# Inverse roots by Ln and Exp from one table set, without reciprocals on VectorE, and another order of steps, in a hybrid decoder layer

## The reference

```python
def rms_norm(x, g):
    y = x * rsqrt(mean(x * x, axis=-1) + 1e-6)
    return y * g
# ssd: y (T, 512) of a Mamba-2 scan, times silu(z)
# nsa: 8 query heads x 64, 2 KV heads; three branches (means of blocks of 32, selected
#      blocks, a window of 512), each a masked softmax; mixed by sigmoid gates, times silu(z)
mix = concat(rms_norm(ssd, ssd_norm_g), rms_norm(nsa, att_norm_g))   # (T, 1024)
x = x + gate * (mix @ w_out)
y = rms_norm(x, final_g)
```

## Time and profile before

| | us |
|---|---|
| median of 3 runs | 929.72 |
| lowest, highest | 928.70, 930.92 |
| the profiled execution, its whole time | 924.17 |
| its span, first to last instruction | 922.40 |

### The profile page before, as it was taken

The page is one execution under the profiler, slowest core; times in us unless marked ns, Lnnn a source line. Parts: engine busy times, 40 slices in busy tenths (PEclk is TensorE's granted clock), DMA queues, the critical chain, the costliest instruction groups (busy, mean ns, idle before and its releaser), DMA issues. The chain is left out here.

```text
span 922.4 us, 18991 instructions
## 1 busy us (share of the span) xinstructions
PE 855.8 (93%) x8117; PEld 499.1 (54%) x8117; DVE 455.9 (49%) x954; ACT 353.4 (38%) x714; POOL 201.0 (22%) x174
## 2 busy tenths in 40 slices
PE   2999999999999999999899998789898989899887
PEld 1454674455566655667455555545556564654553
DVE  1133131052535355446554536886886868667511
ACT  3041000210201044555343236775665656454523
POOL 1001766000200033334410110137210130303021
PEclk9999999999999999999999999789999999999989
DMA  8937137322220000120844541720011010102102
GB/s 281 351 122 280 62 131 248 157 92 91 92 93 0 1 6 0 36 57 1 308 149 130 165 165 35 233 63 27 14 47 50 13 54 18 61 3 69 60 2 91
DMA packets 44461, 88.98 MB, mean 96 GB/s; under 512 B 4196, under 2 KB 25900, under 8 KB 43034
## 3 DMA queue, kind: packets, MB, share of 16 engines
q1 hardware_dynamic: 39354, 56.02, 18.7%
q0 software_dynamic: 5024, 31.75, 9.5%
HBM read 75.49 MB, written 16.40 MB: 100 GB/s over the span
## 5 line engine op out<-in xcount | busy, mean ns | idle before, releaser
L1798 PE MATMUL PS<-hT,W 128*128 128x363 f32 (+1 forms) x384 | 118.6, 469 | 0.0
L1778 PE MATMUL PS<-W,hT 128*128 128x512 f32 x256 | 113.0, 594 | 0.5 <-DVE W L1428 0.5
L1798 PEld LDWEIGHTS PS<-hT,W 128*128 128x128 f32 x384 | 72.2, 189 | 45.6 <-issue 1.7
L1595 DVE CUSTOM_DVE_ANT_0 PS<-PS,consts 128x640 f32<-128x640 f32 (+5 forms) x96 | 77.4, 836 | 29.0 <-PE PS L2107 28.5
L1728 PE MATMUL PS<-W,hT 128*128 128x288 f32 (+1 forms) x256 | 86.5, 500 | 0.0
L1778 PEld LDWEIGHTS PS<-W,hT 128*128 128x128 f32 x256 | 47.9, 190 | 56.3 <-issue 54.8
L886 POOL TENSOR_TENSOR Q<-Q,U 128x512 f32<-128x512 f32 x16 | 20.3, 1266 | 265.8 <-DVE U L1629 265.8
L1728 PEld LDWEIGHTS PS<-W,hT 128*128 128x128 f32 x256 | 48.5, 190 | 37.4 <-issue 30.7
L1155 ACT ACTIVATE hT<-PS,small 128x128 f32<-128x128 f32 (+7 forms) x64 | 46.9, 740 | 49.9 <-DVE small L1595 47.0
L2074 PE MATMUL PS<-U,Y 128*128 128x512 f32 x128 | 60.3, 603 | 0.8 <-ACT OTb L1162 0.8
L2074 PE MATMUL PS<-U,Q 128*128 128x512 f32 x128 | 58.8, 598 | 0.0
(11 more groups left out here) (457 smaller groups left out, 1538.9 us busy)
## 6 DMA issues: line engine op xcount, KB each, us to landing
W<-in_w_in SPq DMA_DIRECT2D x5, 2048.0 KB, 7.9
W<-in_w_ada SPq DMA_DIRECT2D x8, 1024.0 KB, 11.1
U<-in_x_prompt SPq DMA_DIRECT2D x8, 512.0 KB, 7.6
W<-in_w_ada SPq DMA_DIRECT2D x2, 2048.0 KB, 8.0
U<-in_state_win_kv POOLq DMA_DIRECT2D x8, 512.0 KB, 4.9
W<-in_x_prompt SPq DMA_DIRECT2D x8, 512.0 KB, 3.3
out_y_prompt<-W SPq DMA_DIRECT2D x8, 512.0 KB, 2.8
out_new_win_sample<-in_state_win_kv POOLq DMA_DIRECT2D x1, 4032.0 KB, 24.0
```

Of the source, the lines that this page charges most:

```text
L1595: ins = nc.vector.tensor_tensor_reduce(x, x, strip(u), 1.0, -NEG, ALU.add, ALU.min, sneg_m[u % 2][:, m:m + 1])
L1778: ins = nc.tensor.matmul(bank(z_bank(u)), hT3[:, k, i * P:(i + 1) * P], w, start=(k == 0), stop=(k == KT8 - 1))
L1798: ins = nc.tensor.matmul(bank(b, 0, n), w[:, k, ct % 4 * P:ct % 4 * P + P], hT3[:, k, a:a + n], start=(k == 0), stop=(k == KT8 - 1))
```

## The change

It does three things. First, ACT loads, ahead of the stage's first wait, the table set that holds both Ln and Exp. Each inverse root is then computed on ACT alone as exp(-0.5 * ln(scale * x + eps)), in place, by a function `inverse_root`, with a wait for its own instruction after each of the two. Second, DVE's reciprocals, and the semaphores between ACT and DVE for them, go; the final norm's root is no longer taken at a GATE two tiles on or at a ROOT step but at the FINAL itself, and the step h is gone. For the last tile, DVE still adds eps to the first half's sum (now under the semaphore `s_eps_added`) and waits for the finished inverse root. Third, the order of all the steps is another. The diff, without the two hunks that rename and remove semaphores:

```diff
@@ -616,26 +615,26 @@
         LAST_TURN = {UNITS[us[0]][0:2]: n for n, us in enumerate(TURNS)}
 
         MIX = [TT] + list(range(TT))
-        OUTPUT = ("GATE", "SCALE", "TURN", "OUT", "RES", "SQUARE", "ROOT", "FINAL")
+        OUTPUT = ("GATE", "SCALE", "TURN", "OUT", "RES", "SQUARE", "FINAL")
 
 
         NAMES = {"q": "QT", "z": "SAMPLE", "s": "S", "x": "SOFTMAX", "t": "TURNP", "y": "CT", "w": "CV", "v": "PV", "k": "BACK",
-                 "c": "COPY", "m": "SUM", "g": "GATE", "a": "SCALE", "u": "TURN", "o": "OUT", "r": "RES", "n": "SQUARE", "h": "ROOT", "f": "FINAL",
+                 "c": "COPY", "m": "SUM", "g": "GATE", "a": "SCALE", "u": "TURN", "o": "OUT", "r": "RES", "n": "SQUARE", "f": "FINAL",
                  "p": "WGATE"}
         ORDER = (
-            "qqssxsxyxwmtsvcxtqksysxvxcszsxxwkgstmstxvvcsaxykuwsxtmootooogaxtoooqtssrrvxppvctxtskusvxtpvxsvc"
-            "sxoxspsotppxpoxqpkttsnsyorxoogxottosrvvvttcxsknxavsvvvcstxtuwsxxoqsstmkoxxftosstxoxossgoxtxooyrs"
-            "rvxvssfvtvxcaxstxwmkussxxvvststvvxxvsscxqkxosxtosnsoyxosxtstooxwxssrtgoxxossmrxvvxvsastvvtcx"
-            "xkussvvxxtnsxvssfxvsxxsxvyvsstcoxxqwossmotoxosxgstttoxroxaokssrnxvvxvsstvvctxxkussfxvvtvsxvs"
-            "xvxvvssctooxtsxgtxsoxorkssxvvvxsxvvcatytssoxouoxoftrssoxkoooxsnsrwtxoxossgomxxorasxvvstsvvfx"
-            "vtstvxxvvctkuvvnvvvcokoooorogoauofrooonhofroooornhf")
+            "qsqxsxyswxsxstmvcxstqxkzvttcskgasuvvcyoxxowstomxktossxogooxoptarpprquspsvxxtvttspcksxvpxvvcsystxwoso"
+            "gxsmaotpxxypktostooxtssrxtqxonotsrvvvscxtxukwsmxsvxvvsvsxcsototxsxfgstxaoooxtstsxxtotkroossnrxvvvyvx"
+            "cstxkusxsvvvxstsvvxstcxxqostxsoxwsftsxoxosnmsxxorgqtksxsoooyxtsrfsxvvxstasvvxvscxtxkwmusxsvvxssvxxst"
+            "xsvnxvtvcssxooxgtssxxytqooasxstoxsfortxokosrnxvtvsxsvvvxstcsxkusvxxvsvgsvxtxvssxxvvscsttwxomoyxftosw"
+            "soxmoooarxkotrussvxvxvssxvvscoxkoooogaototorsxtsrxvxvsnsnxvvsxtxsvsxsvtvxxvttcfkvvvfvvcukogoaoourooo"
+            "oornooooroofornf")
 
         VALUE_TILES = [min(u // 2, WIN // P if u % 2 else TT) + 1 for u in range(2 * TT)]
         VALUE_STEPS = [u for u, n in enumerate(VALUE_TILES) for _ in range(n)]
         STEPS, seen = [], {}
         for letter in ORDER:
             m = seen[letter] = seen.get(letter, -1) + 1
-            STEPS.append((NAMES[letter], {"o": m // 8, "r": m // 2, "h": TT - 1 + m, "v": VALUE_STEPS[min(m, len(VALUE_STEPS) - 1)]}.get(letter, m)))
+            STEPS.append((NAMES[letter], {"o": m // 8, "r": m // 2, "v": VALUE_STEPS[min(m, len(VALUE_STEPS) - 1)]}.get(letter, m)))
         AGAIN, times = [], {}
         for step in STEPS:
             AGAIN.append(times.get(step, 0))
@@ -643,7 +642,6 @@
         POS = {(what, u, again): n for n, ((what, u), again) in enumerate(zip(STEPS, AGAIN))}
 
 
-        ROOTED = {step: n + 1 for n, step in enumerate(step for step in STEPS if step[0] in ("SCALE", "FINAL") or step == ("SQUARE", TT))}
         ADDED = {step: n + 1 for n, step in enumerate(step for step in STEPS if step[0] in ("BACK", "SQUARE"))}
         TURNED = {step: n + 1 for n, step in enumerate(step for step in STEPS if step[0] in ("CT", "TURNP"))}
 
@@ -1086,6 +1084,13 @@
                 act.activation(PTs[:, 0:4, :].rearrange("p n r -> p (n r)"), bank(0), ACT.Copy).then_inc(s_turned_act, 1)
                 z_silu(Z_AMID[p])
 
+            nc.scalar.preload_act_table_set("natural_log_exp_and_others")
+
+            def inverse_root(to, x, scale, eps):
+
+                alink(act.activation(to, x, ACT.Ln, scale=scale, bias=eps))
+                alink(act.activation(to, to, ACT.Exp, scale=-0.5))
+
             act.wait_ge(s_smp_sum, 4)
             for (what, u), again in zip(STEPS, AGAIN):
                 tile = MIX[u] if what in OUTPUT else None
@@ -1094,7 +1099,7 @@
                     act.wait_ge(s_ysq, 9)
                     q = ssq.rearrange("p (i s) -> p i s", s=2)[:, :, 0:1]
                     for a, b, n in ((0, TT, P), (TT, TT + 1, SR)):
-                        act.activation(q[0:n, a:b], q[0:n, a:b], ACT.Sqrt, scale=1.0 / SW, bias=eps2[0:n]).then_inc(s_yroot, 1)
+                        inverse_root(q[0:n, a:b], q[0:n, a:b], 1.0 / SW, eps2[0:n])
                 if what == "GATE":
 
                     if u:
@@ -1103,28 +1108,26 @@
                         act.wait_ge(s_smp_gated, 1)
                     q = ssq[0:r, 2 * tile + 1:2 * tile + 2]
                     if u:
-                        alink(act.activation(za[tile], Q3[:, tile, :], ACT.Square, accum_out=q))
+                        act.activation(za[tile], Q3[:, tile, :], ACT.Square, accum_out=q).then_inc(s_root, 1)
                     else:
-                        alink(act.activation(za_s, heads(Q3[0:r, tile, :], r), ACT.Square, accum_out=q))
-                    act.activation(q, q, ACT.Sqrt, scale=1.0 / SW, bias=eps2[0:r]).then_inc(s_root, 1)
-                if what == "ROOT" or (what == "GATE" and u > 1):
-                    v = u if what == "ROOT" else u - 2
-                    act.wait_ge(s_squared, v + 1)
-                    f = fss[0:rows(MIX[v]), v:v + 1]
-                    if v == TT:
-                        act.wait_ge(s_squared, TT + 2)
-                        act.wait_ge(s_rooted, ROOTED["SQUARE", TT])
-                        act.activation(f, half_sums[:, 1:2], ACT.Sqrt, scale=1.0 / DM, bias=half_sums[:, 0:1]).then_inc(s_froot, 1)
-                        continue
-                    act.activation(f, f, ACT.Sqrt, scale=1.0 / DM, bias=eps2[0:rows(MIX[v])]).then_inc(s_froot, 1)
+                        act.activation(za_s, heads(Q3[0:r, tile, :], r), ACT.Square, accum_out=q).then_inc(s_root, 1)
+                    act.wait_ge(s_root, u + 1)
+                    inverse_root(q, q, 1.0 / SW, eps2[0:r])
                 if what == "SCALE":
-                    act.wait_ge(s_rooted, ROOTED["SCALE", u])
                     if u > 2:
                         act.wait_ge(xin[tile % 2], 16 + 16 * (tile // 2))
                     for n, M in enumerate((Yt(tile), Q3[:, tile, :])):
                         act.activation(M[0:r], M[0:r], ACT.Copy, scale=ssq[0:r, 2 * tile + n:2 * tile + n + 1]).then_inc(s_scaled, 1)
                 if what == "FINAL":
-                    act.wait_ge(s_rooted, ROOTED["FINAL", u])
+                    f = fss[0:r, u:u + 1]
+                    act.wait_ge(s_squared, TT + 2 if u == TT else u + 1)
+                    if u == TT:
+                        act.wait_ge(s_eps_added, 1)
+                        alink(act.activation(f, half_sums[:, 1:2], ACT.Ln, scale=1.0 / DM, bias=half_sums[:, 0:1]))
+                        act.activation(f, f, ACT.Exp, scale=-0.5).then_inc(s_froot, 1)
+                        act.wait_ge(s_froot, 1)
+                    else:
+                        inverse_root(f, f, 1.0 / DM, eps2[0:r])
                     act.wait_ge(s_added, ADDED["SQUARE", u])
                     if u == TT:
                         act.activation(xres[0][:, 0, :], xres[0][:, 0, :], ACT.Copy, scale=fss[:, u:u + 1]).then_inc(s_final, 1)
@@ -1136,6 +1139,8 @@
                         act.activation(square_junk(u)[:, 2 * n:2 * n + 2], xres[0][:, n, :].rearrange("p (n c) -> p n c", n=2), ACT.Square,
                                        accum_out=half_sums[:, n:n + 1]).then_inc(s_squared, 1)
                 elif what == "SQUARE":
+                    if u:
+                        act.wait_ge(s_squared, u)
                     act.wait_ge(s_summed, 2 * u + 2)
                     act.activation(square_junk(u)[0:r], xrows[u % 2][0:r].rearrange("p (n c) -> p n c", n=4), ACT.Square, accum_out=fss[0:r, u:u + 1]).then_inc(s_squared, 1)
                 if what == "SOFTMAX":
@@ -1550,23 +1555,16 @@
                         dve.wait_ge(s_gated, again + 1)
                         nc.vector.tensor_tensor(x, x, gate_s[again], ALU.add).then_inc(s_summed, 1)
                 if what == "SCALE":
-                    dve.wait_ge(s_root, u + 1)
-                    if u == 0:
-                        dve.wait_ge(s_yroot, 2)
-                    q = ssq[0:r, 2 * tile:2 * tile + 2]
-                    nc.vector.reciprocal(q, q).then_inc(s_rooted, 1)
                     if u == 2:
+                        dve.wait_ge(s_root, 3)
                         nc.vector.tensor_copy(KTx[HALF[0], 0:512], KTs[HALF[1], 0:512]).then_inc(s_swapped, 1)
                         nc.vector.tensor_copy(KTx[HALF[1], 320:], KTs[HALF[0], 320:]).then_inc(s_swapped, 1)
                 if what == "SQUARE" and u == TT:
                     dve.wait_ge(s_squared, TT + 1)
-                    nc.vector.tensor_scalar(half_sums[:, 0:1], half_sums[:, 0:1], 1.0 / DM, EPS, ALU.mult, ALU.add).then_inc(s_rooted, 1)
-                if what == "FINAL":
-                    dve.wait_ge(s_froot, u + 1)
-                    nc.vector.reciprocal(fss[0:r, u:u + 1], fss[0:r, u:u + 1]).then_inc(s_rooted, 1)
-                    if u == TT:
```

(11 more changed lines are left out.)

## The result

The changed kernel takes 934.95 us in the median of 5 runs (933.52 to 937.87), against 929.72 of before in 5 runs taken beside them (926.16 to 930.92). The ratio is 1.0074, with a 95% interval from 1.0040 to 1.0108: some 7 us slower by the ratio, 5 by the medians. The prediction said 9.8 us faster. The profiled execution took 933.52 us, its span is 931.7, where before had 924.17 and 922.40.

The account below looks back on a forecast made before the run. PE was taken as the bound, with some 48 us to win in the last stage. Terms 3.7 + 3.4 + 0.9 + 2.0 - 0.15 gave 9.8 us faster, a median of 920 us, with 8 in 10 for 910 to 931.

Parts of the forecast that it names:

- The rival of the lost table: Table set does not stay loaded, so 20 Ln/Exp pairs bring 40 loads: about 933 us, chance 0.04.
- Small instructions: On ACT, 20 roots become 20 Ln and 20 Exp, at 0.29 us each: 5.8 us more ACT work.
- (a): PE's 1.64 us wait for the stage's first Exp, delayed by a table load: removing it gives back 1.3 us.
- (b): PE's 2.34 us stall at SAMPLE's root, where two loads hold up a softmax: 1.9 us won.
- (c): PE's 0.50 us wait for the first SCALE, behind two more loads: 0.5 us won.
- The tail: At the kernel's end, Ln, a wait and Exp replace Sqrt and reciprocal: about 0.64 us against 0.49, 0.15 lost.
- The clock: In 568 to 627 us PE's low clock costs 10.3 us; a third, 3.4, comes back as idleness goes.
- The later pairs of loads: Six load pairs at prompt tiles' gates lie beside OUT matmuls that keep PE busy: removing them costed at nothing.
- The order: New step order: 0.9 us from one fewer unit-of-v boundary without scores, 2.0 of 3.5 us stalls at the first RES.
- the like count of v: Fronts and ends of v units without scores beside them: two and five before, three and three after; 0.9 us won.
- The margin of the sample's o: The sample tile's first o moves earlier, but w_out's last rows still arrive some 3 us ahead: costed at nothing.
- The rival, order makes DVE wait: Eight more softmax steps right behind their own scores make DVE wait, 12.7 us lost: 932.6 us, chance 0.13.

Follow-up runs that it names:

- e1: The changed kernel with the old order of steps, so only the new roots differ from the kernel before: ratio 0.9982 to before.
- e12: The e1 kernel (new roots, old order) with 20 table loads put back, at SAMPLE's root and each gate's: ratio 1.0004 to before.
- e7: The changed kernel with 14 table loads put back, at the gates from the third prompt tile on: ratio 1.0141 to before.
- e3: The changed kernel with SP's loads of x, gates and final_g held back until the third unit of v is done: ratio 1.0019 to before.
- e5: The e3 kernel (later burst, new order) with 16 small do-nothing transposes ahead of the last stage: ratio 0.9956 to before.
- e6: The e1 kernel (new roots, old order) with 80 small do-nothing transposes ahead of the last stage: ratio 0.9947 to before.
- e11: The e6 kernel with SP's second burst of loads held back as in e3: ratio 0.9936 to before.
- e8: The kernel before, unchanged but for 80 small do-nothing transposes ahead of the last stage: ratio 0.9963 to before.
- e10: The e3 kernel with 88 small do-nothing transposes, the worst place by the count of dense pieces: ratio 1.0104 to before.

## Why the prediction was wrong

**Table kept: right.** The skill's rule (the Trainium skill, "ScalarE: Activation LUTs", Table sets: the hidden batching unit) holds: with the set chosen, Ln and Exp share one load, as the groups of after show. The rival of the lost table is out.

**Small instructions: right, the Exp at the lower bound.** Ln 291 ns, Exp on one column 203, where 290 was taken for both. The difference is no surprise to the Trainium skill ("ScalarE: Activation LUTs", What ACT_TABLE_LOAD costs), which charges each operand read from a column about 93 ns; Ln reads its bias so, Exp does not, and here it is 88.

**Stalls (a), (b) and (c), 3.7 us: wrong in sum.** In the changed kernel the stall at the first Exp is 1.47 us, not 0.3: ACT is idle before it, and the evictions of the turned queries that stand ahead of it (569.12 to 571.52) hold it up, not the load. They start 0.92 us later than before, because in the new string a unit of scores stands ahead of the second q. (c) is 0.24 where it was 0.50. In the old order (a) did shrink to 0.35, as forecast, and (b) became three waits of 3.55 us. The step that failed is to count a stall as won because its releaser gets faster, without asking what is late next.

**The tail, 0.15 us lost: right, and nothing.** Ln starts at 927.20 and Exp ends at 927.73: 0.53 us, where Sqrt and reciprocal took 0.49.

**The clock, 3.4 us: right in size for the first 60 us, by luck.** 10.3 became 6.7 us there. But the term was a third of the loss because part of PE's idleness would go, and that grew, from 10.9 to 17.7 us; why the clock rose all the same is open. Over the whole stage the table has 1.7 us (17.1 to 15.4). It did not reach 0.9 in 590 to 606, where the 5.49 us lie.

**Together: 7.0 us forecast for the roots, tail included; 1.7 us measured (e1, between 4.4 won and 1.1 lost).** The loads alone read 2.0 (e12), no clearer of the noise. One trace of e1 has the clock better by 5.2 us and the fetch worse by 6.4. That fits a PE that runs faster into the ends of its pieces, but e12, with the loads, has 17.5 too; so this split is a reading of single executions, not shown.

**The later pairs of loads at nothing: right for the order of before, wrong for the new one.** In the new one 14 of them cost 6.2 us (e7, give or take 4), 0.44 each. The prediction looked at the cover in the old string and moved the change into another.

**The order, 2.9 us won (0.9 and 2.0): this term decides the sum, and it failed.** From e1 to the changed kernel the order alone costs 8.5 us, give or take 4, where it was to win 2.9. 5.1 of them went with the burst of loads ahead of one fetch (e3). The other 3.4 are not traced to a cause by a run; that they hang on where the boundaries fall is argued from this: with a good place for each, the new order (e5, 0.9956) and the old one (e6, 0.9947) cannot be told apart. Of the two terms themselves, the like count of v came true at the ends: PE's waits for ACT's copies there went from five (2.4 + 0.8 + 0.7 us) to three (2.4 us), 1.5 won; at the fronts the new string has 0.58 and 1.08 behind k z and u. At the first RES the stalls of 1.90 and 1.56 us are gone, and two of the same sum stand in their place, at TURN and at the v behind it:

```profile
619.09 0.66 PE L2045 MATMUL PS<-consts,Y 128*128 128x128 f32 x4 [1.55 <-ACT Q L1120]
...
623.74 3.60 PE L2129 MATMUL PS<-T,Vw 32*64 32x128 f32 x128 [2.07 <-DVE Q L1570]
```

As with (b), other waits took the place of those removed, and the 2.0 us for RES did not come. The prediction counted banks, semaphores and letters; a queue that no letter names, and the number of instructions, were not in it.

**The margin of the sample's o, at nothing: right for o, which did not wait for w_out, and blind for the rest.** The request moved from 591.96 to 590.26 us, and the burst behind it met a fetch of PE. The question was not only who waits for these rows but what shares the DMA with them.

**The rival, order makes DVE wait: the sign was right, the mechanism was not the one.** DVE's waits for scores went from 18 of 28.5 us to 24 of 42.0. But PE's other stalls rose by only 1.5 us. The rival had given 932.6 by its own path.

**A version that beats both.** The new roots in the old order with 80 transposes (e6): 921.5 us, 0.9947 [0.9923, 0.9970]; e11 and e5 are as good. It is clear of before, but not of e1, the roots alone. That place holds for exactly this program: every instruction of PE added or taken out ahead moves it.

## What to carry to other kernels

When PE stands in the middle of a run of small matmuls and the profile names only "issue", number its instructions from stall to stall: a distance of 256 or a multiple is the fetch. It costs where a piece is used up in less than some 3 to 4 us, and more where its packet comes late, as behind a burst of loads (5.49 us against 1.65 with the burst held back). A reordering is not priced until this is looked at, and before it is judged by 1% it should be timed at two or three shifts, since 72 transposes that do nothing moved one order by 13.7 us. A stall ahead of a slow instruction is worth only what remains when the next thing that is late has been found.

## What the runs showed of the hardware that was not expected

- PE's instructions come in 64 DMA packets of 16384 bytes. At the 26 stalls in the traces of before and of the changed kernel the packet took 0.88 to 1.6 us and PE went on 1.25 to 1.51 us behind its end. In 20 of them it began 0.5 to 1.7 us behind PE's entry into the piece ahead, in six 3.3 to 10.2 us, in part with an idle DMA.
- Such a fetch was held up behind bulk loads: with q1 filling the engines it began 6.4 us behind the entry and PE stood 5.49 us; with most of these loads held back it began after 2.5 us and PE stood 1.65.
- 12.8 to 23.9 us of the stage in the 14 traces, up to 2.6% of the kernel, go there, with PE's busy share above 90%.
- Instructions that do nothing, ahead of a stage, made the kernel faster (e5 against e3 by 0.6%, e8 against before by 0.4%) or slower (e10 against e3 by 0.9%).
